# Page numbers loaded ahead of the wait, the last V pages asked for by another queue, and a sum placed behind more products, in a decoder layer kernel

## The reference

```
p  = rmsnorm(x) @ w_in                 # q | k | v | B | C | xv
a  = stick-breaking attention, 8 heads of 64
     prompt: causal, 512 keys
     sample: 8 new keys, then 32 pages of 128 keys for each of 8 sequences,
             newest page first, pages found by page_table
c  = B * conv3(C * xv)
h  = x + concat(rmsnorm(a), rmsnorm(c)) @ w_out
h  = h + cross attention over 256 memory tokens
h  = h + swiglu(rmsnorm(h));  y = rmsnorm(h)
```

## Time and profile before

| | us |
|---|---|
| median of 3 runs | 1175.58 (1172.65 to 1176.09) |
| the profiled execution: time | 1176.88 |
| the profiled execution: span of the trace | 1175.1 |
| PE busy, share of the span | 90% |
| DVE, ACT, POOL busy | 58%, 27%, 35% |
| mean DMA rate over the span | 188 GB/s |

### The profile page before, as it was taken

One profiled execution on the slowest core, in us unless ns is written; L12 is line 12 of the kernel. 1 busy time (PEld: TensorE's weight loads), 2 busy tenths in 40 slices (PEclk: granted clock), 3 DMA queues, 4 the chain that ended last, 5 costly groups with the idle time before them and its releaser, 6 DMA issues.

```text
span 1175.1 us, 28989 instructions
## 1 busy us (share of the span) xinstructions
PE 1062.8 (90%) x11527; PEld 906.1 (77%) x11527; DVE 675.8 (58%) x909; ACT 319.8 (27%) x486; POOL 409.2 (35%) x341
## 2 busy tenths in 40 slices
PE   5899999998688788986799878999999999999997
PEld 3777787775444465654699658999999999999996
DVE  2846657777686778761796449554443014544643
ACT  3512211232233424332522343311221111112121
POOL 0526444443332424443341013343343343334330
PEclk9999999999887899998899999999999999999999
DMA  9979888788998979888431233223212232321222
GB/s 348 348 230 308 287 274 277 252 303 292 353 318 308 375 242 333 295 298 316 154 134 37 77 103 109 72 73 102 76 54 81 81 107 72 98 80 45 69 66 81
DMA packets 126501, 221.16 MB, mean 188 GB/s; under 512 B 9951, under 2 KB 68580, under 8 KB 126388
## 3 DMA queue, kind: packets, MB, share of 16 engines
q1 hardware_dynamic: 103234, 146.63, 36.9%
q0 software_dynamic: 20480, 67.13, 16.3%
q10 hardware_dynamic: 2674, 5.87, 1.3%
HBM read 213.78 MB, written 5.80 MB: 187 GB/s over the span
## 4 chain that ended last, share of the span: by engine, by line
PE 67%; DVE 13%; DMA 8%; issue 4%; SPq 4%; ACT 3%; POOL 1%; POOLq 1%; DVEq 0%; ACTq 0%
PE ps L524 38%; PE ps L1674 11%; PE ps L1777 7%; DMA k_set<-in_cache_sb_k 5%; DVE k_set L1350 3%; PE ps L1828 3%; PE ps L585 2%; SPq L619 2%; SPq L620 2%; DVE r_sq L700 2%; DMA mw_raw<-in_w_in 2%; DVE r_sum L705 1%; DVE om_s L1369 1%; DVE h_lo L429 1%; PE ps L368 1%
## 5 line engine op out<-in xcount | busy, mean ns | idle before, releaser
L480 POOL TENSOR_TENSOR w_lo<-w_raw,w_hi 128x2048 fp32r<-128x2048 f32 (+3 forms) x49 | 193.0, 3941 | 403.8 <-ACT w_hi L457 361.2
L524 PE MATMUL ps<-h_hi,w_hi 128*128 128x288 f32 x832 | 180.1, 298 | 8.7 <-DVE h_lo L429 5.7
L524 PE MATMUL ps<-h_lo,w_hi 128*128 128x288 f32 x832 | 179.1, 297 | 0.0
L524 PE MATMUL ps<-h_hi,w_lo 128*128 128x288 f32 x832 | 179.0, 297 | 0.0
L1350 DVE STREAM_TRANSPOSE k_set<-k_set 128x1024 f32<-128x1024 f32 x128 | 149.5, 1217 | 42.0 <-DMA k_set<-in_cache_sb_k 41.3
L1777 PE MATMUL ps<-k_set,q_blk 32*32 32x256 f32 x4096 | 138.0, 413 | 28.6 <-DVE k_set L1350 27.4
L457 ACT ACTIVATE w_hi<-w_raw 128x2048 fp32r<-128x2048 f32 (+3 forms) x47 | 77.8, 1660 | 256.2 <-PE ps L524 227.2
L524 PEld LDWEIGHTS ps<-h_hi,w_hi 128*128 128x128 f32 x832 | 135.1, 190 | 9.8 <-issue 7.2
L524 PEld LDWEIGHTS ps<-h_hi,w_lo 128*128 128x128 f32 x832 | 135.1, 190 | 0.0
L524 PEld LDWEIGHTS ps<-h_lo,w_hi 128*128 128x128 f32 x832 | 135.1, 190 | 0.0
L1777 PEld LDWEIGHTS ps<-k_set,q_blk 32*32 32x32 f32 x4096 | 79.7, 113 | 71.3 <-DVE k_set L1350 31.1
(11 more groups left out here) (266 smaller groups left out, 1712.6 us busy)
## 6 DMA issues: line engine op xcount, KB each, us to landing
k_set<-in_cache_sb_k SPq DMA_DIRECT2D x256, 256.0 KB, 5.1
v_late<-in_cache_sb_v POOLq DMA_DIRECT2D x152, 256.0 KB, 5.7
v_early<-in_cache_sb_v POOLq DMA_DIRECT2D x96, 256.0 KB, 4.4
mw_raw<-in_w_in SPq DMA_DIRECT2D x12, 1024.0 KB, 6.1
w_raw<-in_w_gate SPq DMA_DIRECT2D x11, 1024.0 KB, 5.4
w_raw<-in_w_up SPq DMA_DIRECT2D x11, 1024.0 KB, 5.3
w_raw<-in_w_down SPq DMA_DIRECT2D x8, 768.0 KB, 4.2
w_raw<-in_w_down SPq DMA_DIRECT2D x8, 640.0 KB, 4.0
```

The source lines that it names most:

```text
L480: return nc.gpsimd.tensor_tensor(w_lo[s][:, ks, :], w_raw[s][:, ks, :], w_hi[s][:, ks, :].bitcast(F32), ALU.subtract)
L524: op = nc.tensor.matmul(ps[:, 2 * t + hf, 0:b - a], weights[s][:, k, t * P:(t + 1) * P], x[:, k0 + k, a:b], start=begin and k == ks[0] and ...
```

## The change

Three edits, in one diff.

1. `load_page` is split. `k_half` loads its eight page numbers into eight registers ahead of its wait, and `v_pages` loads the numbers of all pages that it is called for ahead of the first page's wait. POOL's calls are for groups of four pages; the first call, which was for 12 pages, becomes three calls for four.
2. The last eight V pages are asked for by SP, behind its last K half and ahead of the out projection's first weights, and no longer by POOL in chunk 29.
3. In `gemm_out` the sum over attention's squares stands behind the convolution products of tile 1, where it stood ahead of them.

```diff
@@ gemm_out
                 products(0, 0, True, [k])
+            products(0, 1, True, range(KC))
             rms_pe(pe, "att", sq_a[:, 0, :], T, "conv")
-            products(0, 1, True, range(KC))
@@ page loading
-        def load_page(eng, n, cache, slot, loaded):
-
-            page = eng.value_load(ptb[0:1, n:n + 1], min_val=0, max_val=N_POOL - 1)
+        def page_number(eng, n):
+            return eng.value_load(ptb[0:1, n:n + 1], min_val=0, max_val=N_POOL - 1)
+
+        def load_page(eng, page, cache, slot, loaded):
             eng.dma_start(slot, cache[0, bass.ds(page, 1)].rearrange("o p h d -> p o (h d)")).then_inc(loaded, 16)
@@ k_half
+            first = 64 * (U // 4) + 32 * s + 24 - 8 * (U % 4)
+            numbers = [page_number(sp, first + q) for q in range(8)]
             if H >= 2:
                 sp.wait_ge(m_["half"], H - 1)
             for q in range(8):
-                load_page(sp, 64 * (U // 4) + 32 * s + 24 - 8 * (U % 4) + q, ck, k_set[s][:, q:q + 1, :], s_kp[s][q // 4])
+                load_page(sp, numbers[q], ck, k_set[s][:, q:q + 1, :], s_kp[s][q // 4])
@@ v_pages
+            numbers = {}
+            for n in pages:
+                C, q = divmod(n, 8)
+                numbers[n] = page_number(pool, 64 * (C // 8) + 32 * (q % 2) + 28 - 4 * (C % 8) + q // 2)
             for n in pages:
...
-                load_page(pool, 64 * (C // 8) + 32 * (q % 2) + 28 - 4 * (C % 8) + q // 2, cv, place, loaded)
+                load_page(pool, numbers[n], cv, place, loaded)
@@ SP
+            v_pages(sp, range(8 * CHUNKS - 8, 8 * CHUNKS))
             sp.wait_ge(s_gt, TILES + 8)
             load_stage(sp, "out")
@@ POOL
-            v_pages(pool, range(RING))
+            for n in range(0, RING, 4):
+                v_pages(pool, range(n, n + 4))
...
-                if C == CHUNKS - 3:
-                    v_pages(pool, range(8 * CHUNKS - 8, 8 * CHUNKS))
```

More of the change, by code:

```diff
@@ L656, in v_pages @@
                     pool.wait_ge(s_gt, TILES)
-                C, q = divmod(n, 8)
                 place, loaded, _ = v_place(n)
-                load_page(pool, 64 * (C // 8) + 32 * (q % 2) + 28 - 4 * (C % 8) + q // 2, cv, place, loaded)
+                load_page(pool, numbers[n], cv, place, loaded)
         def pair(t):
```

## The result

The changed kernel takes 1162.7 us, the median of four runs (1159.09 to 1166.56), where the kernel before took 1175.84, the median of four. The ratio is 0.9876, with a 95% interval of 0.9847 to 0.9905: 14.6 us faster, between 11 and 18. A second set, five runs beside a kernel before that took 1176.74, gave 0.9923 (0.9896 to 0.9951), or 9 us. The forecast was 1150: the sign was right, the gain about half of what was forecast in the first set and a third in the second. The measured time lies in the whole range (1133 to 1165), but outside the range of the forecast's own case (1138 to 1157).

A forecast was written before the change was run, and what follows sets the result against it. The page stage was taken as one of turns, no engine full, with SP's queue on the path of K's turns. 12 + 0 + 11 + 3.3 = 26.3 us off 1176.9 gave 1150.6, said as 1150; range 1133 to 1165.

The forecast's parts named there:

- the forecast's own case: Whole kernel: all terms come as forecast, 1150 us, own range 1138 to 1157; chance 0.58.
- Edit 1, SP's side: Page stage: K page numbers at hand let SP ask for the eighth page 4.2 us sooner; 12 us gained.
- That is 13.3 us in five of the stage's 19 asking stretches: Page stage: bytes the DMA engines fail to carry while SP asks slowly, as time at the full 383 GB/s.
- The clock term: Page stage: PE at an unbroken pace keeps its upper clock; lower level loses 25 us, 10 us counted in the upper bound.
- The tile stage: Stage before the pages: PE, busy 196 of 202 us, hides later first pages; 0 lost, at most 4.3 us a half uncovered.
- The first rival: Page stage: K gains nothing because the DMA engines are the bound; edits 2 and 3 remain, 1162 us; chance 0.21.
- The rival of all waits gone: Page stage: all of PE's K waits go, 25.9 us plus some 8 of slow clock; 1129 us; chance 0.11.
- POOL's side: Page stage: grouped V number loads gain 0, from -2 to +2 us, as V is nowhere on the chain.
- Edit 2: Tail: SP asks for the last V pages, chunk 31's sums done 12.4 us sooner; 11 us gained, bounds 6 to 12.4.
- I take off 1.4 us for that: Tail: deduction for w_out's 2 MB standing behind V pages, sharing engines with stores, and ACT's split; leaves 11 us.
- Edit 3: Out projection: moving the sum behind tile 1's convolution products starts tile 2 3.3 us sooner; bounds 0 and 4.6.
- Moved into the idle time they are free: Out projection: 24 convolution products costing 3.2 us fit PE's 4.67 us of idle time ahead of the sum.

The follow-up runs named there:

- K's numbers alone: Kernel before with the eight K page numbers loaded ahead of SP's wait, nothing else: 0.9944, 6.6 us faster.
- The slower asking: Kernel before with each K page number loaded twice on SP, so the eighth page is asked for later: 1186.64 us, 1.0104.
- neither run on V's numbers: V numbers loaded ahead in groups on the kernel before (0.9986); V numbers loaded one by one again on the changed kernel (1164.57 us, 0.9888).
- no mend: Without w_out's first 1 MB asked for ahead of the last V pages (1160.75 us) and without stores moved behind ACT's split of w_out's first weights (1157.37 us).
- w_out first: Changed kernel with w_out's first 1 MB asked for by SP ahead of the last V pages: 1160.75 us, 0.9862.
- the stores later: Changed kernel with ACT's requests for stores of K rows, memory V and convolution state moved behind its split of w_out's first weights: 1157.37 us, 0.9842.
- the edit alone: Kernel before with attention's sum behind the convolution products of tile 1, nothing else: 0.9966, 4.0 us faster.
- V's numbers as before: Changed kernel with POOL's V page numbers loaded one by one again, K's still ahead of the wait: 1164.57 us, 0.9888.
- Making the low part 3.4 us later: POOL's third out-projection low part only after tile 1's evacuation, on the changed kernel with w_out's first 1 MB ahead (1157.95 us) or stores moved back (1159.17 us).

## Why the prediction was right in sign and half in size

**Edit 1, SP's side: forecast 12 us, measured about 5.** The pace of the askings was right: about 0.5 us a page, and where the loads are hidden the eighth is asked for from 3.8 us after the release on. They are not hidden in 4 of the 18 halves: ahead of halves 17, 26 and 29 SP stands at another transfer's wait until the release or until shortly before it, half 18 follows 17, and the eight loads come only then. The first page of these is asked for 3.1 to 5.4 us after the release (before: 0.8 to 1.7), the eighth after 6.7 to 10.0. The failing step is the one that turned missed bytes into time, "That is 13.3 us in five of the stage's 19 asking stretches", and took them at their full worth. Over halves 14 to 31 the last page was asked for 8.8 us after its release before and 5.2 after; from there to its landing it took 8.0 before and 9.9 after (means from the traces' starts). So half of what the asking gained, 1.9 of 3.6 us, went into a longer queue: the eight pages now meet V's pages and each other. V's new groups are not what lengthens it: with K's numbers alone the landing took 9.8 us too. The slower asking shows the same trade the other way: the last page is asked for 13.9 us after the release and lands 5.2 us after that. Of the remaining 1.7 us a half only some turns are on the path. Page stage: mean 253.8 us in the four traces with the old asking, 247.0 in the nine with the new, 6.8 us less. Single traces of one kind lie up to 11 us apart, which is why the first trace's 14 us is not taken for the gain. The clock term that was to come on top is small: the mean clock is 0.93 in the four traces and 0.94 in the nine.

**The tile stage: forecast 0, measured some 1.7 us lost.** Scores 13 end at 278.3 to 280.5 us in the five traces in which SP loads a K number and asks (mean 279.3), and at 279.9 to 283.4 in the nine in which it loads eight ahead (mean 281.0). From 95 to 284 us PE's gaps ahead of the tile products (L1680) that the profile puts to nothing but issue come to 0.5 to 2.5 us in the five of the first kind (mean 1.6), and to 2.1 to 3.9 in the nine of the second (mean 2.8). Why loads on SP's queue should do that was not tried and stays open. With it the term is 6.8 - 1.7 = 5.1 us, beside the 6.6 measured for it alone.

**The first rival.** Its time, 1162, is the first measured median to the us, but that is luck, since its mechanism fell: K's term is not nothing, and the tail's terms are not whole. The Trainium skill, "Trainium Kernel Development and Optimization", Key Constraints, was weighed for it in the prediction: transfers asked for from several engines share the same 16 DMA engines, and asking from several saves issue time only. The traces agree for the full stretches (378 GB/s before, 384 after). In the others the engines were not full, and with the asking sooner the rate rose from 191 to 253 and from 208 to 292 GB/s. The rival of all waits gone fell with PE's 17.7 us of waits that are left. V never came late: from 268 to 520 us PE waited once for V in the changed kernel, for 0.8 us, and neither run on V's numbers moved the time, so the 0 us of POOL's side was right.

**Edit 2: forecast 11 us, measured 5.5.** The first part came: the sums of chunk 31 end 11.4 us sooner (mean of the five traces with the old placing 28.3, of the five with the new and no mend 16.9), where 12.4 was worked out. But 1.6 us of it is chunk 31's sums themselves, which took 1.93 us in place of 3.4 to 3.6 and which the prediction counted; their end is not on the projection's path. That path goes through ACT's copy of the last attention weights, `awT_s`, which starts 14.3 us after the last scores in place of 24.1 (means): 9.8 us sooner. So the first failing step is that term, and the second and larger one is the deduction, "I take off 1.4 us for that". ACT waited 3.7 to 4.8 us for the weights (from `awT_s` to `w_hi` 7.1 us in place of 2.8, on the mean: 4.3 lost), and the projection starts at a mean of 25.0 us in place of 30.5: 9.8 - 4.3 = 5.5. The prediction had named both causes, V pages ahead in SP's queue and the stores, without pricing them by a rate. Moving either away brings the weights: with w_out first no wait is left, with the stores later 0.65 to 1.2 us. The second leaves the V pages ahead of the weights and the sums where they were, so most of the wait was the stores' doing. The bound of 6 us had been the right price for "pages or weights some 5 us late". The signal that was to break the prediction, ACT waiting more than 3 us for w_out, came in all five traces with this placing and no mend.

**Edit 3: forecast 3.3 us, kept about 0.6.** Tile 2 came 3.1 us sooner with the edit alone, by the steps given, but 2.5 us sooner in the changed kernel. "Moved into the idle time they are free" counted on 4.67 us of idle time ahead of the sum. In the changed kernel PE stands 6.4 us ahead of the projection and makes its first 24 products in 5.4 us, where they took 3.4, so that 2.3 us are left for a block of 3.2, and the sum starts 0.7 us later behind its input (0.8 and 1.2 in the two like traces). The second step that failed, and the larger, is that nothing was asked of what stands behind tile 0's evacuation. In the kernel before its addition took 0.76 us (584.87), and the DVE instruction that met POOL's low part was tile 1's squaring (588.04, 4.25 us), behind the xT that PE waits for: tile 3 came at PE's own pace, 6.4 us after tile 2.

```profile
584.90 1.93 ACT L457 ACTIVATE w_hi<-w_raw 128x2048 fp32r<-128x2048 f32 x1 [9.89 <-PE ps L585]
...
586.90 4.77 POOL L480 TENSOR_TENSOR w_lo<-w_raw,w_hi 128x2048 fp32r<-128x2048 f32 x1 [9.94 <-ACT w_hi L457]
...
588.04 4.25 DVE L700 TENSOR_TENSOR r_sq<-xT 128x576 f32<-128x576 f32 x1
```

POOL's low part follows ACT's split, which waits for PE's products of tile 1. These now come sooner after the sum by more than a block of 3.2 us, so the low part starts 9.6 us after the sum in place of 14.4, while tile 0's evacuation starts after 6.6 in place of 9.2. The low part moved further than the evacuation, and it is tile 0's addition that meets it, and takes 5.05 us ahead of tile 1's evacuation. So tile 3 is now set by the end of POOL's work: 570.84 for POOL, 571.44 for DVE. The Trainium skill, "SBUF — State Buffer", Who interferes with whom, says that a DVE instruction with two SBUF inputs contends with a GpSimd instruction that reads SBUF, and that the order of issue decides which of them is blocked. This case agrees, in the three traces shown (5.05, 5.04 and 5.04 us): POOL was first each time (here 566.23 against 566.39), and DVE ended 0.6 us after it. Counted from the sum's input, tile 3 comes after 18.0, 18.2 and 18.5 us in the changed kernel's two traces and that with V's numbers as before, against 18.8 before: 0.6 us on the mean. That may be the clock alone: in the two traces with the old order in which the sum took 1.21 us and not 1.74, tile 3 stands at 17.0 us after the sum already (17.2 after the input), no later than with the new order. Making the low part 3.4 us later gives 1.7 us.

**The sum.** 5.1 + 0 + 5.5 + 0.6 = 11.2 us, where 26.3 was forecast. The two measurements of the changed kernel are 14.6 (11 to 18) and 9 (6 to 12).

## What to carry to other kernels

An asking made sooner is worth only what the transfer engines have room to carry: take the gain from the time between release and landing, not from the release to the last asking, and expect half back where the queues are full. When a stall in a tail is removed, price what comes next by the rate and by everything that shares it, stores among them; here stores of 1.93 MB in 8 us, cut to 0.55, brought a wait of 4 us down to about 1. And when an instruction is moved to start sooner, look at which long GpSimd instruction the next VectorE ones will meet, and whether the same move brings that one sooner too. Take the gain from when the inputs are ready, not from when the moved instruction starts.

## What the runs showed of the hardware

The instruction with which SP asks for a page took 0.33 us, and it was 1.10 us once in a run of eight (342.93). The askings for w_out were slower still, in the changed kernel's group of that line (ns least, median and longest, then the first and last start):

```profile
L449 SPq DMA_DIRECT2D w_raw<-in_w_out x3: 367/1528/4613, 527.1 to 550.9; - x3
```

The first two, right behind the eight V pages, are the ones of 1.5 and 4.6 us. With V's numbers as before, where the same eight pages are asked for over a longer time, they took 0.44 and 0.62 us. So an asking seems to be held up itself when many transfers are out; that was not tried alone. With q10 and q1 both loaded, the 3.18 MB in 8 us come to 397 GB/s, above the 383 that the prediction took as full. The same code differed by 7.4 us in the page stage of two executions (241.7 us at a granted clock of 0.951, 249.1 at 0.931). The medians of their two sets differ by 7.0 us, where those of the kernel before beside them differ by 0.9.
